# Seven places for value pages, output split during the last pair, softmax in halves: a paged sparse attention layer in float32

## What is computed

```python
def mixer_block(h, ...):
    (q, k, v, iq, ik, iw, hq, hf, hi, hg, ga, gb) = jnp.split(h @ w_in, IN_OFFSETS, axis=-1)
    attn = attend(q, k, v, iq, ik, iw, pos)          # prompt, or the 8 requests over a paged cache
    o, s_new = hgrn2_chunked(...)
    o = rms_norm(o, o_norm) * silu(hg)
    merged = sigmoid(ga) * (attn @ w_proj_attn) + sigmoid(gb) * (o @ w_proj_hgrn)
    return merged @ w_out, ...
# attend, for a request: logits of q with all 2048 cached keys plus 8 new ones, not chosen ones at -inf,
# softmax over them, and the weighted sum of the cached and new values
```

## Time and profile before

| | us |
|---|---|
| median of 3 runs | 1807.91 (1807.11 to 1810.99) |
| profiled execution, its own time | 1808.42 |
| its span, first to last instruction | 1806.8 |
| TensorE busy | 1668.3 (92%) |
| stage of the 8 requests, first turn to last `rows_turn` | about 219 |

### The profile page before, as it was taken

One profiled execution on the slowest core, in us unless ns is written; L12 is line 12 of the kernel. 1 busy time (PEld: TensorE's weight loads), 2 busy tenths in 40 slices (PEclk: granted clock), 3 DMA queues, 4 the chain that ended last, 5 costly groups with the idle time before them and its releaser, 6 DMA issues. The chain is left out here.

```text
span 1806.8 us, 29148 instructions
## 1 busy us (share of the span) xinstructions
PE 1668.3 (92%) x12749; PEld 1525.3 (84%) x12753; DVE 726.7 (40%) x1184; ACT 448.9 (25%) x629; POOL 696.3 (39%) x584
## 2 busy tenths in 40 slices
PE   7999999999998999677899968885899999999998
PEld 6999999999857999565787745554899999999998
DVE  6332012234255797675665423332554323012221
ACT  4121111222442143001233323331233212112111
POOL 3334444455303355741234342221243433444342
PEclk9999999999998999886899989996999999999999
DMA  6232333333402132110332167886432322323222
GB/s 172 71 94 61 90 107 94 104 94 92 149 8 90 61 93 85 47 50 26 131 97 76 57 267 270 350 352 242 178 94 71 94 70 70 97 81 93 68 76 85
DMA packets 193502, 203.59 MB, mean 113 GB/s; under 512 B 6224, under 2 KB 179344, under 8 KB 184928
## 3 DMA queue, kind: packets, MB, share of 16 engines
q1 hardware_dynamic: 173040, 105.56, 20.4%
q0 software_dynamic: 12832, 80.29, 11.7%
q10 hardware_dynamic: 7504, 15.88, 2.4%
HBM read 187.21 MB, written 14.30 MB: 112 GB/s over the span
## 5 line engine op out<-in xcount | busy, mean ns | idle before, releaser
L472 POOL TENSOR_TENSOR w_lo<-raw,w_hi 128x512 fp32r<-128x512 f32 (+1 forms) x398 | 525.9, 1351 | 822.0 <-ACT w_hi L617 822.0
L1529 PE MATMUL ps<-n_lo,w_hi 128*128 128x288 f32 x1824 | 544.5, 299 | 1.0 <-ACT qT L723 1.0
L1530 PE MATMUL ps<-n_hi,w_lo 128*128 128x288 f32 x1824 | 539.1, 296 | 0.0
L1531 PE MATMUL ps<-n_hi,w_hi 128*128 128x288 f32 x1824 | 537.4, 295 | 0.0
L1529 PEld LDWEIGHTS ps<-n_lo,w_hi 128*128 128x128 f32 x1824 | 342.6, 188 | 15.3 <-issue 14.5
L1531 PEld LDWEIGHTS ps<-n_hi,w_hi 128*128 128x128 f32 x1824 | 344.2, 189 | 0.0
L1530 PEld LDWEIGHTS ps<-n_hi,w_lo 128*128 128x128 f32 x1824 | 343.2, 188 | 0.1
L617 ACT ACTIVATE w_hi<-raw 128x2048 fp32r<-128x2048 f32 (+2 forms) x108 | 187.9, 1740 | 270.0 <-PE ps L1531 267.9
L1529 PE MATMUL ps<-hid_lo,w_hi 128*128 128x288 f32 x704 | 209.0, 297 | 0.0
L1530 PE MATMUL ps<-hid_hi,w_lo 128*128 128x288 f32 x704 | 207.9, 295 | 0.0
L1531 PE MATMUL ps<-hid_hi,w_hi 128*128 128x288 f32 x704 | 207.2, 294 | 0.0
(11 more groups left out here) (294 smaller groups left out, 2305.1 us busy)
## 6 DMA issues: line engine op xcount, KB each, us to landing
raw<-in_ffn_w_gate SPq DMA_DIRECT2D x44, 512.0 KB, 4.0
raw<-in_ffn_w_up SPq DMA_DIRECT2D x44, 512.0 KB, 5.2
raw<-in_ffn_w_down SPq DMA_DIRECT2D x32, 704.0 KB, 4.6
raw<-in_w_in SPq DMA_DIRECT2D x22, 1024.0 KB, 5.3
scratch_g<-g_out POOLq DMA_DIRECT2D x8, 576.0 KB, 3.1
gates<-scratch_g ACTq DMA_DIRECT2D x4, 1152.0 KB, 8.8
raw<-in_w_out SPq DMA_DIRECT2D x4, 1024.0 KB, 5.1
scratch_x<-xT ACTq DMA_DIRECT2D x1, 2304.0 KB, 12.1
```

Of the source, the lines that this page charges most:

```text
L472: ins = pool.tensor_tensor(w_lo[:, u % NRAW, part], raw[:, u % NRAW, part], w_hi[:, u % NW, part].bitcast(F32), ALU.subtract)
L1529: pe.matmul(dst, hi, x_lo, start=first, stop=False)
L1530: pe.matmul(dst, lo, x_hi, start=False, stop=False)
L1531: return pe.matmul(dst, hi, x_hi, start=False, stop=last)
```

## The change

It does seven things, all in the stage above.

1. V_RING is 7: three places stay (`v_here`), four lie over `n_hi` and `n_lo` (`v_more`), which are free once the last gate unit is multiplied. Groups 6, 5 and 4 are gathered before and during the gate loop, group 0 right after it.
2. Gate output 7 has a place of its own (`g_last`); GpSimd no longer waits for the last gate store before the gathers, and makes the low part of the projections' unit 1 in the middle of the last pair, not before gate output 7.
3. The turns of a pair's group 1 come before the transposes of the previous pair's probabilities, not after.
4. The maximum over banks 0 and 1 is taken after key group 5, that of bank 2 after group 7 (`maxima_of`), bank 3 and the new keys at the end. The exponential is done in two halves of 1024 with a semaphore each.
5. The transposed probabilities are copied by ScalarE (0, 2, 4) and DVE (1, 3).
6. `oT` is cut, and the prompt's part of `aT`, on DVE ahead of the last pair's `rows_out`; the requests' 64 columns of `aT` follow `heads_out`. TensorE begins the projections with both halves of the recurrence's part and needs `aT` only after them. In the other units, too, the recurrence's part comes first.
7. ScalarE issues the loads of the gates while the last pair's values are multiplied (`GATES_AT` places the first where memory is free first).

```diff
@@ attention_pages (GpSimd)
+                value_group(6)
                 for n in range(8):
-                    lows(at_unit["gate", n] + 2)
+                    lows(min(at_unit["gate", n] + 2, at_unit["proj", 0]))
+                    if n == 6:
+                        pool.wait_ge(S("gate_stored1"), 48)
+                        value_group(5)
+                    if n == 7:
+                        pool.wait_ge(S("gate_stored0"), 64)
+                        value_group(4)
...
-                for m in range(2):
-                    pool.wait_ge(S(f"gate_stored{m}"), 64)
...
+                pool.wait_ge(S("unit_done"), at_unit["gate", 7] + 1)
+                value_group(0)
+                for m in range(K_RING, K_RING + 9):
                     key_group(m)
+                    if m - K_RING < 3:
+                        value_group(m - K_RING + 1)
                 for pair in range(1, 4):
+                    key_group(8 * pair + 4)
                     for n in range(LEFT if pair > 1 else 0):
-                        value_group(8 * pair - 8 - LEFT + n)
-                    key_group(8 * pair + 1)
+                        value_group(8 * pair - 8 - LEFT + n + V_RING)
                     for n in range(1, 8):
...
+                        if 8 * pair + n + 4 < 32:
+                            key_group(8 * pair + n + 4)
+                        if n <= 8 - LEFT:
+                            value_group(8 * pair - 8 + n - 1 + V_RING)
+                        if pair == 3 and n == 3:
+                            lows(at_unit["proj", 1])
@@ loads of the gates (ScalarE)
-            act.wait_ge(S("aT_done"), 4)
             for g in range(DC // 2):
...
+                if g == 0:
+                    act.wait_ge(S("sp_turned"), 20)
+                else:
+                    act.wait_ge(S("v_used"), 4 * (25 + g))
@@ maxima (DVE)
+                def maxima_of(pair, at, first, banks):
+
+                    dve.wait_ge(S("kp_used"), 8 * pair + 2 * (first + banks))
...
+                    link(dve.tensor_reduce(stat[:, at:at + 1], flat[:, 512 * first:512 * (first + banks)], AX_X, ALU.max))
@@ end of sample_attention (DVE)
                 heads_out(2)
+                dve.wait_ge(S("kp_turned"), 128)
+                link(dve.tensor_copy(o_hi[:, :, :], oT[:, :, :]))
+                dve.tensor_tensor(o_lo[:, :, :], oT[:, :, :], o_hi[:, :, :].bitcast(F32), ALU.subtract).then_inc(S("o_split"), 1)
+                a_split(slice(NS, T))
                 rows_out(3)
                 heads_out(3)
                 dve.wait_ge(S("aT_done"), 4)
+                a_split(slice(0, NS))
@@ projections (TensorE)
                     if g == 0:
-                        pe.wait_ge(S("mix_split"), 8)
+                        pe.wait_ge(S("o_split"), 1)
+                        part(1, 0)
+                        part(1, 1)
+                        pe.wait_ge(S("a_split"), 2)
                     for a in range(2):
                         if g:
                             pe.wait_ge(S("merged"), 2 * g + a - 1)
...
+                            part(1, a)
+                        part(0, a).then_inc(S("unit_done" if a else "proj_half"), 1)
```

More of the change, by code:

```diff
@@ L913, in sample_attention @@
                     turned(pair - 1)
-                    for g in range(8 * pair + 1, min(8 * pair + 9, 32)):
+                    for g in range(8 * pair + 2, min(8 * pair + 10, 32)):
                         keys(g)
@@ L1434, in heads_out, with a_split, keys_of @@
                     ins.then_inc(S("aT_done"), 1)
-                for g in range(9):
-                    keys(g)
+                def a_split(part):
+                    dve.wait_ge(S("kp_used"), 32)
+                    link(dve.tensor_copy(a_hi[:, :, part], aT[:, :, part]))
+                    dve.tensor_tensor(a_lo[:, :, part], aT[:, :, part], a_hi[:, :, part].bitcast(F32),
+                                      ALU.subtract).then_inc(S("a_split"), 1)
+                def keys_of(pair, first):
+                    for g in range(first, min(8 * pair + 9, 32)):
+                        keys(g)
+                        if g == 8 * pair + 5:
+                            maxima_of(pair, 16, 0, 2)
+                        if g == 8 * pair + 7:
+                            maxima_of(pair, 17, 2, 1)
+                        if pair >= 2 and g == 8 * pair + 4:
+                            heads_out(pair - 2)
+                keys_of(0, 0)
                 for pair in range(1, 4):
                     maxima(pair - 1)
+                    keys(8 * pair + 1)
                     if pair >= 2:
                         rows_out(pair - 2)
+                    turned(pair - 1)
                     inverse(pair - 1)
-                    for g in range(8 * pair + 1, min(8 * pair + 9, 32)):
-                        keys(g)
-                        if pair >= 2 and g == 8 * pair + 4:
-                            heads_out(pair - 2)
+                    keys_of(pair, 8 * pair + 2)
                 maxima(3)
                 rows_out(2)
+                turned(3)
                 inverse(3)
                 heads_out(2)
+                dve.wait_ge(S("kp_turned"), 128)
+                link(dve.tensor_copy(o_hi[:, :, :], oT[:, :, :]))
+                dve.tensor_tensor(o_lo[:, :, :], oT[:, :, :], o_hi[:, :, :].bitcast(F32), ALU.subtract).then_inc(S("o_split"), 1)
+                a_split(slice(NS, T))
                 rows_out(3)
@@ L2056, in sample_attention @@
                 for pair in range(1, 4):
+                    for hp in range(4):
+                        turn(32 * pair + 4 + hp)
                     if pair >= 2:
@@ L2064, in sample_attention @@
                         prob_turn(pair - 1, j)
-                    pe.wait_ge(S("spT_done"), 5 * pair)
-                    for hp in range(4):
-                        turn(32 * pair + 4 + hp)
                     new_values(pair - 1)
```

151 lines of the change are left out of this document (86 added, 65 removed).

## The result

The changed kernel took 1764.04, 1761.65 and 1753.31 us, a median of 1761.65, against 1807.51 of the kernel before in the same series: a ratio of 0.9732, 95% interval 0.969 to 0.9774. A fourth run, in the slower state, took 3169.78 us and is left out of all that follows. Two more series of it, six runs each, gave 1759.08 (ratio 0.9713, 0.9683 to 0.9744) and 1763.18 (0.9728, 0.9703 to 0.9753). The forecast was 1760, with a range of 1748 to 1776. The execution profiled first took 1764.04 us, with a span of 1762.2.

What follows compares the result with a forecast made beforehand. TensorE's idle time and slow clock in the requests' stage were taken as the bound, the DMA second. Savings of 7.2 + 14.7 + 3.9 + 1 + 21 = 47.8 us from 1808.4 gave 1760 us, range 1748 to 1776.

Steps and rivals of the forecast that it cites:

- What bounds the kernel: Requests' stage, 229.1 us: TensorE's idle time and slow clock limit it, the DMA at 421 GB/s comes second.
- Start: Stage's beginning: first gather 9.7 us earlier, less 2.5 for one extra value group; 7.2 us saved, bounds 4.7 to 9.7.
- Transitions: Between pairs: 14.5 us falls to 9.4 or 9.7, saving 14.7; the last, 11.75 to 7.9, saves 3.9.
- Middles: Pairs between transitions: value waits go, but the DMA has little air; 1 us gained, bounds 5 gained to 8 lost.
- rival A: Gathers set the pace of the pairs: 9 to 14 us less saved, about 1772 us; chance 0.17.
- End: Last values to projections: 33.7 us becomes 12.1; 21 us saved after 0.4 back at the first merge, bounds 15 to 24.
- stall on group 31: In the end: the last value group shares the DMA with gate loads and lands at 9.8, a stall of 2.7 us.
- The rule on the port: At the end: DVE's cast of `oT` could delay group 31's gather by at most 1.8 us; by the trace row, nought.
- D: Seven value places bring little, since keys hold TensorE; start and cuts give the rest, about 1787 us; chance 0.08.
- E: Slower: value gathers ahead of keys in one queue delay each key group 2.49 us, 72 in all, 1832 us; chance 0.03.
- B: Gate loads take the DMA from group 31 and TensorE's clock drops: 6 + 1.4 us more, about 1768; chance 0.08.
- C: Larger gain: gathers keep up, no stall, warm start; 4 + 3 + 3 us more, about 1750; chance 0.12.

Runs made afterwards that it cites:

- late_start: Changed kernel with unit 1's low part back ahead of the last gate output and GpSimd waiting for all gate stores before its gathers: 1771.62 us, ratio 0.9789.
- keys_first: Changed kernel with GpSimd's gathers behind the gate outputs reordered, two value groups fewer ahead of keys 5 to 8: 1756.36 us, ratio 0.9702.
- before_again: The kernel before the change, unedited, profiled a second time: 1810.23 us, ratio 0.9998.
- after_again: The changed kernel, unedited, profiled a second time: 1759.08 us, ratio 0.9713.
- turns_behind: Changed kernel with the four turns of key group 8p+1 put back behind the turns of the probabilities: 1770.27 us, ratio 0.9769.
- three_places: Changed kernel with three value places instead of seven, no groups gathered in the gate loop, later gate loads behind the last value group: 1772.09 us, ratio 0.9792.
- no_cover: Changed kernel with the projections' recurrence half also waiting for the cuts of the attention's outputs: 1761.58 us, ratio 0.9739.
- gates_last: Changed kernel with all four of ScalarE's gate loads waiting until value group 31 has landed: 1753.42 us, ratio 0.9684.
- after: The changed kernel, unedited, in its first series and profile: 1761.65 us, ratio 0.9732.
- after_third: The changed kernel, unedited, profiled a third time: 1763.18 us, ratio 0.9728.
- late_cuts: Changed kernel with all cuts of o and a made in one piece each behind the last heads: 1770.63 us, ratio 0.9776.

## Why the prediction came out right, point by point

**What bounds the kernel** was read rightly: TensorE's idle time in this stage went from 58.7 us (229.1 - 170.4) to 19.3 (176.1 - 156.8), and with it the clock rose; what follows the stage is the same to 0.4 us in these two profiles. (The prediction's 169.7 us of busy time leaves out the 0.73 of the last stretch of the earlier trace rows.)

**Start**, 7.2 forecast, 6.7 read (45.9 to 39.2); late_start and keys_first show it as 10.3 won and 3.4 given back. Value groups 6, 5 and 4 cost nothing, as forecast: TensorE has no wait for weights in the gate loop or the prompt attention.

**Transitions**, 14.7 + 3.9 forecast, 18.2 read: 14.5, 14.6, 14.5 and 11.75 became 9.1, 10.3, 9.8 and 7.97. The waits for the exponential are 2.0 us, the clock 1.00 where it was 0.76 and 0.88. The working of 9.4 and 9.7 is off by at most 0.6 in each.

**Middles**, 1 forecast, 6.6 read (31.6, 33.6, 28.95 to 30.0, 29.9, 27.7), and 2.7 by the third profile (30.6, 32.4, 28.5), which is of a chip with long middles. The two profiles of chip 4 give 6.5: 30.5, 33.1 and 30.1 in before_again, 29.8, 29.9 and 27.4 in after_again. This is the one term that was mis-sized, and rival A had even the other sign. The step was "a pair of about 9.7 + 31 = 40.7 us asks for gathers of 39.8, which leaves the DMA 0.9 us of air", with the fear that the DMA would set the pace. The first two pairs came out at 39.1 and 40.2 us (9.1 + 30.0, 10.3 + 29.9), from 1128.0 to 1178.0 at 418 to 420 GB/s without a break, and TensorE had no key wait in the second middle at all. The term had counted 2.5 us of value waits as gone, and set nearly all of it against losses that did not come. In before_again the middles hold 5.8 us of value waits and 0.4 of key waits, in after_again neither: that is the term on one chip. What I did not see is that the early turns free a key place before the softmax, so that the gathers run through the transition (share 1.01 after, 0.69 and 0.66 before, 0.78 in turns_behind); the middles before had paid for that gap. I had put the steady flow down to the places for values, and three_places, with 0.6 us of value waits in its three middles, shows that the pairs hardly need these.

**End**, 21 forecast, 21.6 read (33.7 to 12.13), and by the table's marks 21.6, 18.7 and 21.5 in the three profiles (34.2 to 12.5, 15.4, 12.6). The inner terms: stall on group 31 of 2.7 forecast, 2.1, 3.7 and 2.5 in the three profiles; projections after 12.1, 12.13 read; 0.4 before the first merge, 0.6 read; cover by the recurrence's half, as no_cover shows. The places' part of it is 11.5 us and the cuts' 8.9. That the two streams share the DMA is shown by gates_last. One reading was off: group 31 alone is not "just in time at 7.4", since seven groups are done after 6.8 us (7.8 x 7/8); the 0.6 us between is the wait that gates_last keeps.

**The rule on the port.** The Trainium skill (SBUF — State Buffer, "Who interferes with whom") says that copies and casts on DVE can take a port pair that GpSimd needs, and the prediction applied this to the cast of `oT` and the gather of group 31. In the first profile of after the gather is issued in 0.94 us, at 1215.91, just behind the cast, and by the row alone the push was nought. But in after_again TensorE did group 24 in 1.08 us instead of 1.94, the gather met the cast and took 1.59: it ended at 1216.44, 0.80 behind the cast. So trace and rule agree; the push is 0.65 us, within the bound of 1.8, and it decides nothing: the gather's data had the gates' loads ahead of it.

**Rivals.** A, D and E fell: key waits of 1.9 us in all behind the first pair (7.2 - 5.3), a stage 53 shorter, no time above before. Of D it stayed true that the pairs hardly need the places. B was right in its mechanism and not in its price: the gates' loads take the DMA from group 31 for 1.5 to 3 us, not 7.4. C came nearest in the stage of the first profile (53.0 of its 57.8), with the stall still in it; in the other two (50.4 and 49.0) the forecast did.

**The sum**: 47.8 forecast, and 53.0, 50.4 and 49.0 in the three stages of after against 229.1 (50.8 to 54.8 against the second profile of before). The profiled executions of after lost 8 to 9 us ahead of the stage, which no step of mine foresaw, and so the first two profiled executions lie 44.4 apart. Over the runs the three ratios give 48.4, 51.9 and 49.3 us (0.0268 and 0.0287 of 1807.5, 0.0272 of 1811.9), each with an interval of 5 to 8 us to either side. The size of the gain was thus forecast as well as the runs can tell; that the medians of 1759 to 1763 fall on 1760 is in part luck, as the middles gave more than forecast and the late beginning took some of it back in an unknown share of the runs.

What stays open: why the clock ahead of the stage has two patterns and what picks one, and why the second middle takes 29.9 us in some profiles and 31.7 to 32.4 in those of chips 5 and 8. In the latter TensorE is both longer at work (30.3 us of that middle in after_third, 29.7 in after) and longer idle: its waits for `kpT` copies by ScalarE are 5.2 us in all in after_third and 3.2 in after, with the same copies at the same 0.60 and 0.69 us.

## What to carry to other kernels

Turn or use the next block's operand before a softmax or another serial step, not behind it: this fills the engine, keeps its clock, and frees a ring's place, so that the gathers run through the step. Give more buffers to the stream whose last groups nothing else hides; in the steady part three were as good as seven. Loads that nobody needs soon go behind the last gather that somebody waits for, and in one queue the operand that is needed first goes first.

## What the runs showed of the hardware that was not expected

GpSimd's issue of a gather (0.94 us) can be held up by DVE's work on SBUF, and not by casts alone. In three_places, where three gathers are issued during the cuts, DVE and GpSimd:

```profile
1207.70 1.36 DVE L1514 CAST o_hi<-oT 128x2304 fp32r<-128x2304 f32 x1
1208.28 1.61 POOL L511 DMA_INDIRECT v_here<-in_cache_v,kv_row  x1 [5.25 <-PE ps L2111]
1209.09 2.56 DVE L1515 TENSOR_TENSOR o_lo<-oT,o_hi 128x2304 fp32r<-128x2304 f32 x1
...
1210.19 2.72 POOL L511 DMA_INDIRECT v_here<-in_cache_v,kv_row  x1 [0.30 <-PE ps L2111]
...
1212.82 2.29 DVE L1486 TENSOR_TENSOR a_lo<-aT,a_hi 128x2048 fp32r<-128x2048 f32 x1
1213.21 2.72 POOL L511 DMA_INDIRECT v_here<-in_cache_v,kv_row  x1 [0.30 <-issue]
```

The first ends 0.83 us behind the cast (1209.06 to 1209.89), the last 0.82 behind the subtraction (1215.11 to 1215.93). The second, begun in the subtraction, ends 0.12 behind the cast that follows it (1211.57 to 1212.79). A subtraction doesn't always hold a gather: in after, and in seven other profiles, the gather of group 31 begins 0.04 to 0.05 us into the subtraction and takes its 0.94, and the subtraction 2.63 instead of 2.56.

TensorE also stood still in the middle of a value group with nothing in the profile that it waited for: 1.79 us in after_again, 1.78 in turns_behind and 1.2 in late_cuts. These are the three profiles with the gates' four loads at their place beside the values in which group 24 took 1.08 us; where it took 1.94, or where the loads come later, no such gap is there. Why is not known; the gather was held in the first two and not in late_cuts.
